# A fused mixer and retrieval kernel: two rows of eight built by GpSimd, an inverse kept by transposes, and an earlier order at the start and in the first mixer

## What is computed

```
h  = x;  xn = rms_norm(h)
proj = xn @ w_in                      # hq, hf, hi, hgate, gq, gk, gv, glow, ggate
o  = chunked gated linear attention   # 4 + 4 heads: q k^T with exp(cum_i - cum_j), then times v
h += (norm(o) * silu(gate)) @ w_out
# retrieval: 8 heads, 2 x 128 sub-keys, 16 experts per head and token out of 128 x 128
g  = softmax(top 16 of sums);  h += sum_k g_k gelu(h . u[e_k]) v[e_k]
# second layer: delta rule (chunks with an inverse of a unit lower triangular matrix),
# spatial gating, window attention, attention on a memory, gates, output
L  = strict lower part of (beta k) k^T * decay
sol = triangular_solve(I + L, rhs)
```

## Time and profile before

| | us |
|---|---|
| median of 3 runs | 1471.51 |
| lowest, highest | 1470.42, 1471.89 |
| the profiled execution, its own time | 1472.0 |
| its span | 1470.2 |

### The profile page before, as it was taken

One profiled execution on the slowest core, in us unless ns is written; L12 is line 12 of the kernel. 1 busy time (PEld: TensorE's weight loads), 2 busy tenths in 40 slices (PEclk: granted clock), 3 DMA queues, 4 the chain that ended last, 5 costly groups with the idle time before them and its releaser, 6 DMA issues.

```text
span 1470.2 us, 22385 instructions
## 1 busy us (share of the span) xinstructions
PE 1430.2 (97%) x8002; PEld 1229.4 (84%) x8002; DVE 1011.8 (69%) x1817; ACT 733.6 (50%) x1113; POOL 98.3 (7%) x112
## 2 busy tenths in 40 slices
PE   8998999999999999999999999999999999999998
PEld 8877878688788888888888888888889899888786
DVE  6577479899866666666666666666668564665565
ACT  5544322276555555555555555555555832465343
POOL 0052134400000000000000000000010100000000
PEclk9999999999999999999999999999999999999999
DMA  5432253111365555555565556555534432334442
GB/s 202 176 118 83 89 212 129 43 58 44 129 198 188 186 187 194 188 186 190 190 191 185 187 192 190 187 188 188 181 138 174 165 135 87 137 131 148 170 169 101
DMA packets 56297, 229.16 MB, mean 156 GB/s; under 512 B 6689, under 2 KB 6961, under 8 KB 47409
## 3 DMA queue, kind: packets, MB, share of 16 engines
q1 hardware_dynamic: 55776, 228.19, 45.5%
q10 hardware_dynamic: 464, 0.20, 0.0%
HBM read 226.27 MB, written 2.10 MB: 155 GB/s over the span
## 4 chain that ended last, share of the span: by engine, by line
PE 89%; DVE 4%; ACT 3%; DMA 2%; issue 1%; POOL 0%; ACTq 0%; DVEq 0%; POOLq 0%
PE ps L2206 23%; PE ps L2016 15%; PE ps L2195 13%; PE ps L1983 8%; PE ps L2193 8%; PE ps L1940 5%; PE ps L2181 4%; PE ps L2159 2%; PE ps L2191 2%; PE ps L2056 1%; DVE lo L1349 1%; ACT hi L863 1%; PE ps L1951 1%; PE ps L2317 1%; PE ps L2327 1%
## 5 line engine op out<-in xcount | busy, mean ns | idle before, releaser
L1558 DVE TENSOR_TENSOR lo<-raw,hi 128x1024 fp32r<-128x1024 f32 x238 | 290.9, 1222 | 62.7 <-ACT hi L1003 62.7
L2195 PE MATMUL ps<-x,hi 128*128 128x512 f32 x840 | 301.9, 398 | 0.0
L1003 ACT ACTIVATE hi<-raw 128x1024 fp32r<-128x1024 f32 x238 | 250.1, 1051 | 0.0
L2193 PE MATMUL ps<-x,lo 128*128 128x256 f32 x960 | 249.7, 281 | 0.0
L2016 PE MATMUL ps<-hi,x 128*128 128x512 f32 x704 | 225.9, 395 | 4.9 <-ACT big L1111 2.5
L1349 DVE TENSOR_TENSOR lo<-raw,hi 128x2048 fp32r<-128x2048 f32 x62 | 142.5, 2300 | 80.8 <-ACT hi L863 80.7
L2193 PEld LDWEIGHTS ps<-x,lo 128*128 128x128 f32 x960 | 181.6, 189 | 9.3
L2195 PEld LDWEIGHTS ps<-x,hi 128*128 128x128 f32 x840 | 157.8, 188 | 33.6
L1050 ACT ACTIVATE oi<-ps 128x256 f32<-128x256 f32 x120 | 46.2, 385 | 234.6 <-PE ps L2195 233.4
L2016 PEld LDWEIGHTS ps<-hi,x 128*128 128x128 f32 x704 | 133.0, 189 | 34.9 <-ACT big L1111 3.0
L2206 PE MATMUL ps<-hi,wh 128*128 128x512 f32 x496 | 154.2, 392 | 3.6 <-DVE wl L1568 2.6
(11 more groups left out here) (382 smaller groups left out, 2157.9 us busy)
## 6 DMA issues: line engine op xcount, KB each, us to landing
raw<-in_v_t SPq DMA_DIRECT2D x128, 512.0 KB, 3.5
raw<-in_u_t SPq DMA_DIRECT2D x126, 512.0 KB, 3.4
raw<-in_pieces SPq DMA_DIRECT2D x62, 1024.0 KB, 4.8
ring<-in_peer_w_q SPq DMA_DIRECT2D x4, 2048.0 KB, 9.5
big<-in_up SPq DMA_DIRECT2D x4, 2048.0 KB, 8.6
ring<-in_w_mem_kv SPq DMA_DIRECT2D x2, 2048.0 KB, 8.4
resid<-in_x SPq DMA_DIRECT2D x1, 1024.0 KB, 5.4
big<-in_mem SPq DMA_DIRECT2D x1, 1024.0 KB, 4.9
```

What stands on the lines that cost most here:

```text
L1003: act.activation(hi[:, which, par], raw[:, which, par], ACT.Copy).then_inc(hi_done[which], 1)
L1558: dve.tensor_tensor(lo[:, which, par], raw[:, which, par], hi[:, which, par].bitcast(F32), ALU.subtract).then_inc(lo_done[which], 1)
L2193: pe.matmul(first, u_lo[:, par, c], xh[:, c], start=False, stop=False)
L2195: ins = pe.matmul(both, u_hi[:, par, c], x2[:, :, c], start=False, stop=(c == KC - 1))
```

## The change

- **Start:** x comes in two halves and piece hq0 in two halves, all issued at once, without a wait for the parameters. Rounding and low part of hq0 and of x go by halves. VectorE scales x before it looks at the parameters, and the three clears move between the low parts of later pieces. The small exp of the lower bounds moves behind the rounding of hq1.
- **First mixer:** `scores(0, ...)` stands between hi and gv, VectorE keeps them before the low part of hgate0, and ScalarE takes the first exp ahead of the outputs of gv.
- **Retrieval:** ScalarE takes the exp of the softmax ahead of the output of mv1.
- **G:** GpSimd makes rows 6 and 7 of hotB in each group.
- **Inverse:** X is no longer updated. TensorE transposes the new Z in the middle of the level's piece, and ScalarE copies it to X.

```diff
@@ sync @@
-            sp.dma_start(resid[:], t["x"]...).then_inc(x_then_norm_f_loaded, 16)
+            for n, loaded in enumerate((x0_then_norm_f_loaded, x1_then_out_stored)):
+                sp.dma_start(resid[:, n], t["x"][0, n * P:(n + 1) * P, :]).then_inc(loaded, 16)
+            sp.dma_start(raw2[:, 0, 0:D], t["pieces"][0][:, 0:D]).then_inc(hq0a_then_mkv_moved, 16)
+            sp.dma_start(raw2[:, 0, D:2 * D], t["pieces"][0][:, D:2 * D]).then_inc(tile_loaded[0], 16)
-            sp.wait_ge(params_loaded, 64)
-            for k in range(NP1):
+            for k in range(1, NP1):
                 load_piece(k)
@@ gpsimd @@
+            pool.wait_ge(pickT_done, 2)
+            for g in range(NG):
+                if g >= GBUF:
+                    pool.wait_ge(g_mm, 2 * (g - GBUF) + 2)
+                for k in range(GRP - POOL_ROWS, GRP):
+                    at = slice(g * GRP + k, g * GRP + k + 1)
+                    ins = pool.tensor_scalar(hotB[:, g % GBUF, k], iota, chosenT[:, 1, at], chosenT[:, 2, at], ALU.is_equal, ALU.mult)
+                ins.then_inc(masks_then_pool_rows_done, 1)
@@ scalar @@
-            piece_split_hi("hq0")
-            copy_hi_T(0, C_N1)
+            act.wait_ge(hq0a_then_mkv_moved, 16)
+            act.activation(hi2[:, 0, 0:D], raw2[:, 0, 0:D], ACT.Copy).then_inc(hq0a_hi, 1)
+            copy_hi_T(0, C_N1, range(HALF))
+            act.wait_ge(tile_loaded[0], 16)
+            act.activation(hi2[:, 0, D:2 * D], raw2[:, 0, D:2 * D], ACT.Copy).then_inc(piece_hi, 1)
+            copy_hi_T(0, C_N1, range(HALF, KC))
             piece_split_hi("hq1")
...
             split_2nd_after("gv0")
+            level_decay(0)
             for a in range(NT):
                 out_group(f"gv{a}", vtok[:, a, TILE:D], ACT.Copy)
...
             for k, g in enumerate(("mk0", "mk1", "mv0", "mv1")):
+                if g == "mv1":
+                    act.wait_ge(soft_in, 1)
+                    e = best.rearrange("p n h k -> p (n h k)")
+                    act.activation(e, e, ACT.Exp).then_inc(soft_exp, 1)
                 out_group(g, mkv_new..., ACT.Copy)
...
+                if l < LEVELS - 1:
+                    act.wait_ge(z_transposed, l + 1)
+                    act.activation(flat(X), ps[:, 6:8, :].rearrange("p b n -> p (b n)"), ACT.Copy).then_inc(x_done, 1)
@@ vector @@
-            mark(dve.memset(own, 0.0)); mark(dve.memset(qd, 0.0)); mark(dve.memset(kd, 0.0))
...
-            piece_split_lo("hf1", "gqk0")
+            mark(dve.memset(own, 0.0))
+            piece_split_lo("hf1")
+            mark(dve.memset(qd, 0.0))
+            piece_split_lo("gqk0")
+            mark(dve.memset(kd, 0.0))
             dve.wait_ge(group_out, group_no["hf1"] + 1)
...
-            piece_split_lo("gv1", "hgate0")
+            piece_split_lo("gv1")
+            dve.wait_ge(masks_then_pool_rows_done, 1)
+            keep(0, masks[:, LEVELS])
+            piece_split_lo("hgate0")
...
-                for k in range(1, GRP):
+                for k in range(1, GRP - POOL_ROWS):
...
-                    if l < LEVELS - 1:
-                        dve.tensor_tensor(X[:, part], X[:, part], ps[:, 6 + n, :]..., ALU.subtract).then_inc(x_done, 1)
@@ tensor @@
-            for name in ("hi", "gv"):
-                token_pieces(name)
+            token_pieces("hi")
             pe.wait_ge(softplus_done, 1)
             pe.wait_ge(fgate_done, 1)
             scores(0, qF, kF)
+            token_pieces("gv")
...
                     pe.wait_ge(onehot_ready, n + 1)
+                    if half:
+                        pe.wait_ge(masks_then_pool_rows_done, g + 2)
...
-                    if l < LEVELS - 1:
-                        for th in range(DH * n, DH * n + DH):
-                            ins = pe.matmul(th_out(6, th), Z[:, th], Y[:, th], start=True, stop=True)
...
+                def transpose_new_z(tile):
+                    if tile and l < LEVELS - 1:
+                        pe.wait_ge(z_done, NT * l)
+                        for th in range(TH):
+                            ins = pe.transpose(th_out(6, th), Z[:, th], ident[:])
+                        ins.then_inc(z_transposed, 1)
-                    token_piece(piece, banks, g2_done)
+                    token_piece(piece, banks, g2_done, transpose_new_z)
```

More of the change, by code:

```diff
@@ L43 @@
 ROUNDS = 4
+POOL_ROWS = 2
 FULL = 4
@@ L565, in build @@
         out_done = sem("out_done")
-        stored = sem("stored")
+        hq0a_hi = sem("hq0a_hi")
+        x1_then_out_stored = sem("x1_then_out_stored")
         groups2 = ["dnq0", "dnq1", "dnk0", "dnk1", "dnv0", "dnv1", "dnz0", "dnz1", "ba", "gmu0", "gmu1", "gmv0", "gmv1",
@@ L686, in _ @@
                     sp.wait_ge(qk_mm, 1)
-                    sp.dma_start(mkv, t["mkv_keep"]).then_inc(mkv_moved, 16)
+                    sp.dma_start(mkv, t["mkv_keep"]).then_inc(hq0a_then_mkv_moved, 16)
                 if loaded_pieces[k] in UP_AFTER:
@@ L816, in _ @@
             act.dma_start(gnorm[:, 1], t["gla_norm_g"][0].partition_broadcast(P)).then_inc(params_loaded, 16)
-            act.wait_ge(x_then_norm_f_loaded, 16)
-            for n in range(NT):
+            for n, loaded in enumerate((x0_then_norm_f_loaded, x1_then_out_stored)):
+                act.wait_ge(loaded, 16)
                 act.activation(sqtmp[:, n], resid[:, n], ACT.Square, accum_out=sumsq[:, n:n + 1]).then_inc(sumsq_done, 1)
             act.wait_ge(params_loaded, 64)
-            act.wait_ge(lb_in_then_sum, 1)
-            act.activation(lbe.rearrange("p a f -> p (a f)"), lbe.rearrange("p a f -> p (a f)"), ACT.Exp).then_inc(lb_exp_then_rest_out, 1)
             def copy_out_T(n_before, dst, gcol=None, first=4):
@@ L833, in copy_out_T, with copy_hi_T @@
                     ins.then_inc(actT_done[0], 1)
-            def copy_hi_T(n_before, gcol):
-                for c in range(KC):
+            def copy_hi_T(n_before, gcol, chunks=range(KC)):
+                for c in chunks:
                     act.wait_ge(transposed, n_before + c // 2 + 1)
@@ L914, in _ @@
             split_2nd_after("gv1")
-            for l in range(LEVELS):
-                act.wait_ge(lvl_exponent, l + 1)
-                act.activation(feat(dec[:, l % 2]), feat(dec[:, l % 2]), ACT.Exp).then_inc(lvl_decay, 1)
+            for l in range(1, LEVELS):
+                level_decay(l)
                 if 1 <= l <= 4:
@@ L1301, in wait_marked @@
                 dve.wait_ge(dve_step, steps[0])
-            mark(dve.memset(own, 0.0))
-            mark(dve.memset(qd, 0.0))
-            mark(dve.memset(kd, 0.0))
+            for n in range(NT):
+                dve.wait_ge(rstd_done, 1 + n)
+                dve.tensor_scalar(scaled[:, n], resid[:, n], rstd[:, n:n + 1], None, ALU.mult).then_inc(scaled_done, 1)
             dve.wait_ge(params_loaded, 64)
@@ L1310, in _ @@
             dve.tensor_tensor(lbe, logit, bcast(lbm, 1, 2), ALU.subtract).then_inc(lb_in_then_sum, 1)
-            for n in range(NT):
-                dve.wait_ge(rstd_done, 1 + n)
-                dve.tensor_scalar(scaled[:, n], resid[:, n], rstd[:, n:n + 1], None, ALU.mult).then_inc(scaled_done, 1)
-            dve.wait_ge(params_loaded, 64)
             def copy_out_T(n_before, dst, gcol=None, first=4):
@@ L1326, in copy_out_T, with copy_lo_T @@
                     ins.then_inc(actT_done[1], 1)
-            def copy_lo_T(rounded_before, gcol):
-                for c in range(KC):
+            def copy_lo_T(rounded_before, gcol, chunks=range(KC)):
+                for c in chunks:
                     dve.wait_ge(actT_done[0], rounded_before + 2 * (c // 2) + 2)
@@ L1349, in piece_split_lo @@
                     dve.tensor_tensor(part_of(lo2, name), raw_piece(name), part_of(hi2, name).bitcast(F32), ALU.subtract).then_inc(piece_lo, 1)
-            piece_split_lo("hq0")
-            copy_lo_T(0, C_N1)
+            dve.wait_ge(hq0a_hi, 1)
+            dve.tensor_tensor(lo2[:, 0, 0:D], raw2[:, 0, 0:D], hi2[:, 0, 0:D].bitcast(F32), ALU.subtract)
+            copy_lo_T(0, C_N1, range(HALF))
+            dve.wait_ge(piece_hi, 1)
+            dve.tensor_tensor(lo2[:, 0, D:2 * D], raw2[:, 0, D:2 * D], hi2[:, 0, D:2 * D].bitcast(F32), ALU.subtract).then_inc(piece_lo, 1)
+            copy_lo_T(0, C_N1, range(HALF, KC))
             piece_split_lo("hq1")
@@ L1410, in _ @@
                 if l == 0:
-                    dve.wait_ge(masks_done, 1)
                     piece_split_lo("hgate1")
-                keep(l, masks[:, LEVELS if l == 0 else l - 1])
+                else:
+                    keep(l, masks[:, l - 1])
                 if 1 <= l <= 4:
@@ L1972, in need_split @@
             def need_split(name, chunks=KC):
-                pe.wait_ge(piece_lo, piece_no[name] + 1)
+                if name != "hq0":
+                    pe.wait_ge(piece_lo, piece_no[name] + 1)
                 return tuple(v[:, piece_slot(name)].rearrange("p (c n) -> p c n", c=chunks) for v in (hi2, lo2))
@@ L1996, in token_tile, with feature_piece @@
```

(2 more changed lines are left out.)

49 lines of the change are left out of this document (23 added, 26 removed).

## The result

The changed kernel takes 1454.4 us (median of 4 runs, 1453.45 to 1457.26) beside 1471.7 us for the kernel before (4 runs, 1470.42 to 1471.9). The ratio is 0.9888, 95% interval 0.987 to 0.9905. Measured again in another session it was 1455.2 us beside 1470.5, ratio 0.9896 (0.988 to 0.9913). 1453.0 was predicted, with the range 1449 to 1461.

What follows compares the result with a forecast made beforehand. TensorE, busy 1430.2 of 1470.2 us, was taken to bound the kernel, and VectorE stage G. Terms 1.4 - 0.3 + 5.4 + 8.3 + 4.5 = 19.3 us off 1472.0 gave 1452.7, rounded to 1453; range 1449 to 1461.

Steps and rivals of the forecast that it cites:

- Start, -1.4: Start of the kernel: first product at 14.9 in place of 16.32, saving 1.4 us, bounds 0 and 1.5.
- Third clear, +0.3: Clears between low parts: the third, 2.62 us, makes the low part of gqk1 late, costing 0.3 us (0 to 0.9).
- First mixer, -5.4: First mixer: gaps ahead of gv0 and level 0's scores go, and the lower clock; 5.4 us saved, bounds 1.9 and 5.6.
- the lower clock behind it: First mixer, scores of level 0: 5.05 us at lowered clock behind the gap would become 3.27, saving 1.8 us.
- Picks, -0.4: Picks ahead of G: earlier softmax exp, but first distance waits for mkv's store; 0.4 us saved, bounds 0.4 and 2.1.
- Picks and G together, -8.3: Picks and G: TensorE becomes the bound at 2.65 us per group; 8.3 us saved, bounds 0 and 10.4.
- Inverse, -4.5: Inverse: transposes replace the second products, 0.9 us saved in each of five levels, 4.5 in all, bounds 0 and 4.6.
- Rival 1: VectorE stays the bound of G, group 2.75 to 2.95 us; G gives 0 to 5, time 1456 to 1461; chance 0.17.
- Rival 2: In G, whole VectorE and GpSimd instructions exclude each other; VectorE's group 3.0 to 3.24, time 1463 to 1470; chance 0.1.
- Rival 3: Start or first mixer gives half; 3 to 4 us missing, time 1456 or 1457; chance 0.1.
- Rival 5: In G, a row costs GpSimd over 1.7 us, so GpSimd sets G and the kernel is slower than before; chance 0.03.

Runs made afterwards that it cites:

- e4_params_first: Changed kernel, but SyncE waits for the four parameter loads before issuing the second piece (hq1); 1453.38 us, ratio 0.988 to the kernel before.
- e7_clears_back: Changed kernel with the three clears (own, qd, kd) again at the head of VectorE's queue; 1453.69 us, ratio 0.9881 to the kernel before.
- e3_scores_back: Changed kernel with the first mixer's order (diagonal scores, first decay, first keep) as before; 1457.81 us, ratio 0.9908 to the kernel before.
- the second profile: Profile of the unmodified changed kernel, run once more beside the experiments; median 1455.18 us, ratio 0.9896 to the kernel before, profiled execution 1453.59 us.
- e1_rows_back: Changed kernel with GpSimd's two rows per group of hotB back on VectorE, early softmax exp kept; 1463.02 us, ratio 0.9943 to the kernel before.

## Why the prediction was right, and where not

The total was right: 1453.0 predicted, 1454.4 and 1455.2 measured. The sum of the steps was 19.3 us, and 15.3 to 17.3 were measured. The 2 to 4 us too much stand in the start, the clear, the first mixer and the inverse. The sizes below are from the traces, except for the first mixer.

1. **Start, -1.4.** The keep-busy calls, transposes and first product came as worked out: 14.9 said, 14.73 and 15.08 measured. The step that failed is "they are wanted at about 10, and landed at 6.7": the parameters landed at 11.95, since they now share with the pieces. The first half of hq0 was late too, at about 10.2 and not "by 8.9". The next half of the product waits again, and e4_params_first shows that 1.6 us hang on the megabyte that is issued with them. With the clears at the head (e7_clears_back) the whole start gives 55.57 against 56.18, which is 0.6.
2. **Third clear, +0.3.** It was 1.1 (55.57 against 56.66; all three clears moved, and net of the later scaling of x), beyond my upper bound of 0.9. The row of VectorE that I used was right, but each clear also has 0.59 us of issue time ahead of it, which the earlier trace rows show and which I left out.
3. **First mixer, -5.4.** The gaps went as said, and they are worth 2.0 to 3.7, by the clock ahead of them. The 1.8 for "the lower clock behind it" was mis-sized: e3_scores_back has the gap and no lower clock behind it. From hi0 to the second square the second profile is 86.36 against 91.81, the predicted 5.4, but the first profile of the same kernel is 88.85, which is 3.0. That the second one meets the prediction is luck of the clock.
4. **Picks, -0.4.** Right as a first step, and for the reason given: the first distance waits for the store of mkv, and the low clock moves from the chunks to the first groups. It is 0.41 in e1_rows_back (100.23 - 99.82).
5. **Picks and G together, -8.3.** Right in size, 8.0 to 8.25, and TensorE is the bound at 2.65 (75.00 us busy of 75.00). But GpSimd's row was "0.3 to 0.5", and it is 0.79 to 0.86 by itself. And I let the blocks fall on VectorE ("2.42 to 2.95"), while they fell on GpSimd, which waits out the comparison. Two rows of 0.8 and a pause fit into 2.65, so the size came out right although the price of the row and the place of the blocks were wrong, and that is luck. How much room was left no run shows; one row more is 18 us slower.
6. **Inverse, -4.5.** 3.67. Levels 2 to 5 gave the 0.9 each that was said. Level 1 gave 0.07, because there Z isn't "subtracted about 4.3 into a level" but after 1199.04 - 1193.11 = 5.9, behind two low parts; its wait of 0.58 explains that much of the missing 0.8, and the rest stays open.

Rival 1 (VectorE stays the bound) is ruled out by VectorE's unchanged durations at the shorter period, and by TensorE, which is busy all the time. Rival 2 (whole instructions exclude each other) has the right mechanism and the wrong victim. I argued against it with 1.08 us from the earlier trace rows, and that argument fell: GpSimd does wait for all that is left of the comparison. What kept it harmless is that GpSimd's rows don't stop VectorE's small rows, which are 0.347 beside 0.365 before. Rival 3 came about at the start. Rival 5 would have decided at 1.67 us for a row; the mean was 1.34, but 0.8 of it is the row and the rest is the pause.

The parts as the experiments size them are 8.1 for picks and G, 3.7 for the inverse, about 3 for the first mixer and -0.5 for start and clears (the first value piece at +0.48): 14.3, beside 15.3 to 17.3 for the whole. The remainder of 1 to 3 us is of the size of what the clock takes or gives in single runs, and isn't resolved.

## What to carry to other kernels

- Work moved to an idle engine is priced by that engine's own row for that very form and by who shares a port with it. Its busy time doesn't tell how much room is left: GpSimd was busy for 75.00 of 75.00 us here, of which about 1.0 in each 2.65 was a pause behind VectorE. Look at the engine that should be the bound, and try one piece of work more and one less.
- A low clock seen behind a gap in one profile isn't the gap's price. Undo the part, or take a second profile, before counting it. And a low clock ahead of a wait hides in it, until the wait is filled.
- Transfers issued earlier also delay the small loads that share the engines with them. Ask which small load the first instruction waits for.

## What the runs showed of the hardware

- GpSimd's comparison with two scalars per partition takes 0.79 to 0.86 us for 128 elements, beside 0.29 and 0.41 us for the other forms of that length. While VectorE compares two SBUF inputs (1.23 us), it stands still: 1.63, 1.81 and 2.10 us, according to how much of the comparison is left. The comparison isn't held, even where GpSimd's row starts 0.53 us before it (2.25 us for the row, 1.21 for the comparison).
- GpSimd's clears of 3072 elements hold up a VectorE product of one tensor with one scalar per partition: 5.72 us for 0.75. That VectorE form runs 1024 elements in 0.75 us, where the comparison of two inputs needs 1.23 for as many. The Trainium skill (SBUF — State Buffer, SBUF: two separate sides) names a VectorE instruction in a two-port mode as one that is excluded by a GpSimd instruction that started first. The trace agrees with that order (8.21 and 8.30); that this form runs in such a mode is suggested by its 0.75 us alone.
- The granted clock at the same place of the same program was 0.76 in one profile and 1.00 in another, with equal waits in the 34 us ahead of it, for 1.6 us of difference.
